# Moving modulation groups, squares and roots inside the loop over the recurrence's heads, in a two-block kernel on one core

## The reference, cut to what matters

```python
mod = (sc @ ada_w[l] + ada_b[l])[:, None, :]     # 9 rows of 1024: shift, scale, gate three times
...
hm = merge_heads(mlstm_chunkwise(q, k, v, log_i, log_f))                   # 4 heads of 128
out_m = head_rmsnorm(hm, mnorm_g, MLSTM_HEADS) * jax.nn.sigmoid(mo.astype(f32))
...
ho = merge_heads(hgrn2_chunkwise(hq_, hk_, hv_, hlf))                      # 4 heads of 128
out_h = head_rmsnorm(ho, hnorm_g, HGRN_HEADS) * jax.nn.silu(hg.astype(f32))
merged = jnp.concatenate([out_m, out_h], axis=-1).astype(y.dtype)
return merged @ w_out
```

## Time and profile before

| | |
|---|---|
| median of 3 runs | 1725.26 us (1725.07 to 1725.27) |
| profiled execution, its own time | 1724.61 us |
| span of the profiled execution | 1722.8 us |
| granted clock of PE over the span | 0.999 |
| loop (first `attend` to first transposition of the merged rows) | 346.55 to 386.04 us |
| busy over the span | PE 97%, DVE 66%, ACT 46%, POOL 21% |

### The profile page before, as it was taken

One profiled execution on the slowest core, in us unless ns is written; L12 is line 12 of the kernel. 1 busy time (PEld: TensorE's weight loads), 2 busy tenths in 40 slices (PEclk: granted clock), 3 DMA queues, 4 the chain that ended last, 5 costly groups with the idle time before them and its releaser, 6 DMA issues.

```text
span 1722.8 us, 32701 instructions
## 1 busy us (share of the span) xinstructions
PE 1678.9 (97%) x12702; PEld 1496.3 (87%) x12702; DVE 1142.6 (66%) x1883; ACT 789.4 (46%) x1239; POOL 354.7 (21%) x325
## 2 busy tenths in 40 slices
PE   6999999999999999999899999999999999999997
PEld 3999879977999889878779999999999988888886
DVE  4877867787555556874663899488899644444445
ACT  4433455655544454632243544555544433333334
POOL 2000100111000100000010767500000155555554
PEclk9999999999999999999999999999999999999999
DMA  9878855427565544430045455555555566666665
GB/s 361 291 268 306 303 226 180 147 103 277 172 216 173 195 137 145 155 131 11 27 171 173 125 175 179 164 159 159 159 161 158 177 191 193 193 195 192 189 193 169
DMA packets 64960, 314.40 MB, mean 182 GB/s; under 512 B 7216, under 2 KB 7632, under 8 KB 45776
## 3 DMA queue, kind: packets, MB, share of 16 engines
q1 hardware_dynamic: 63504, 305.94, 53.7%
q10 hardware_dynamic: 1280, 6.82, 1.1%
q0 software_dynamic: 64, 0.04, 0.0%
HBM read 311.72 MB, written 1.05 MB: 182 GB/s over the span
## 4 chain that ended last, share of the span: by engine, by line
PE 91%; DVE 3%; DMA 2%; ACT 1%; issue 1%; POOL 1%; SPq 0%; POOLq 0%; DVEq 0%; ACTq 0%
PE bank L421 26%; PE bank L423 25%; PE bank L422 25%; PE bank L2906 2%; DMA ring<-in_stream 2%; PE bank L2879 1%; DMA ring<-in_experts 1%; PE bank L2465 1%; PE bank L1447 1%; DVE ring_rounded L381 1%; PE bank L2478 1%; PE bank L857 1%; POOL ring_rounded L3212 1%; PE bank L2118 1%; PE bank L2132 0%
## 5 line engine op out<-in xcount | busy, mean ns | idle before, releaser
L423 PE MATMUL bank<-yb_rounded,ring_rounded 128*128 128x256 f32 x2032 | 574.8, 283 | 0.0
L2997 ACT CAST ring_rounded<-ring 128x1024 fp32r<-128x1024 f32 x248 | 260.5, 1051 | 287.1 <-DMA ring<-in_experts 287.1
L423 PEld LDWEIGHTS bank<-yb_rounded,ring_rounded 128*128 128x128 f32 x2032 | 389.5, 192 | 0.0
L381 DVE TENSOR_TENSOR ring_rounded<-ring,arena_rounded 128x1024 fp32r<-128x1024 f32 x230 | 272.8, 1229 | 105.2 <-ACT arena_rounded L367 104.5
L421 PE MATMUL bank<-yb_rounded,arena_rounded 128*128 128x256 f32 x1104 | 315.5, 286 | 2.2 <-issue 1.9
L422 PE MATMUL bank<-yT_rounded,arena_rounded 128*128 128x256 f32 x1104 | 312.6, 283 | 0.0
L3172 DVE TENSOR_TENSOR ring_rounded<-ring,ring_rounded 128x1024 fp32r<-128x1024 f32 x128 | 156.9, 1226 | 191.4 <-ACT ring_rounded L2997 191.4
L421 PE MATMUL bank<-yb_rounded,ring_rounded 128*128 128x256 f32 x960 | 278.2, 290 | 1.3 <-POOL ring_rounded L3212 0.5
L422 PE MATMUL bank<-yT_rounded,ring_rounded 128*128 128x256 f32 x960 | 271.3, 283 | 0.0
L367 ACT CAST arena_rounded<-ring 128x1024 fp32r<-128x1024 f32 x230 | 229.1, 1048 | 88.0 <-PE bank L421 77.5
L422 PE MATMUL bank<-ring_rounded,arena_rounded 128*128 128x512 f32 x688 | 268.0, 390 | 0.0
(11 more groups left out here) (447 smaller groups left out, 2608.3 us busy)
## 6 DMA issues: line engine op xcount, KB each, us to landing
ring<-in_stream SPq DMA_DIRECT2D x140, 1024.0 KB, 4.9
ring<-in_experts SPq DMA_DIRECT2D x256, 512.0 KB, 3.6
field<-in_stream SPq DMA_DIRECT2D x28, 512.0 KB, 7.1
field<-in_stream SPq DMA_DIRECT2D x4, 1024.0 KB, 8.4
yT<-in_stream SPq DMA_DIRECT2D x4, 512.0 KB, 5.5
field<-in_gains ACTq DMA_DIRECT2D x3, 512.0 KB, 7.9
field<-in_gains ACTq DMA_DIRECT2D x1, 1536.0 KB, 7.9
const<-in_const SPq DMA_DIRECT2D x1, 1473.0 KB, 11.8
```

Of the source, the lines that this page charges most:

```text
L381: ins = nc.vector.tensor_tensor(ring_r[:, g % SLOTS, half], ring[:, g % SLOTS, half], top.bitcast(F32), ALU.subtract)
L423: return first, pe.matmul(bank, s_rest, m_top, start=False, stop=stop)
L2997: nc.scalar.copy(expert_top[:, n % E_SLOTS, :], expert_w[:, n % E_SLOTS, :]).then_inc(expert_top_ready, 1)
```

## The change

It moves four things inside the loop; nothing is added or removed.

1. PE: in passes 2 and 4 the modulation groups stand ahead of `attend(i)` and `read_out(i - 1)`, not behind them. ACT's copy of their bank moves to match, to just behind `decay_exp(i + 1)`.
2. ACT: the eight squares of the mLSTM are taken four in pass 2 and four in pass 3, behind that pass's `head_square`, not all in pass 1 ahead of it.
3. ACT: the roots of the mLSTM are taken in pass 4, not pass 2.
4. DVE: their inverse is taken in pass 5, not pass 3.

```diff
@@ mix_pe
                 if i < HEADS * TT - 1:
                     decays(i + 1)
+                if i in LOOPED:
+                    ada_groups_pe(pe, LOOPED[i])
                 attend(i)
                 if i:
                     read_out(i - 1)
-                if i in LOOPED:
-                    ada_groups_pe(pe, LOOPED[i])
                 if i - 1 in LOOPED:
                     ada_sum_pe(pe, LOOPED[i - 1], but=3)
@@ mix_act
                 if i < last:
                     decay_exp(i + 1)
+                if i in LOOPED:
+                    ada_groups_act(act, LOOPED[i])
                 if i % TT:
                     bank = A.get(act)
                     nc.scalar.copy(cross[:, i // TT % 2, :], bank[:, 0:P]).then_inc(A.free, 1)
-                if i == 1:
-                    act.wait_ge(V.free, 4 + values_end["m"])
-                    for t in range(TT):
-                        for h in range(HEADS):
-                            ins = nc.scalar.activation(square_junk[:, t * HEADS + h, :], dm[:, h, t * P:(t + 1) * P], ACT.Square,
-                                                       accum_out=head_squares[:, t * HEADS + h:t * HEADS + h + 1])
-                    a(ins)
                 if 0 < i < last:
                     head_square(i - 1).then_inc(sem("h_squared"), 1)
                 if i == 2:
+                    act.wait_ge(V.free, 4 + values_end["m"])
+                if i in (2, 3):
+                    t = i - 2
+                    for h in range(HEADS):
+                        ins = nc.scalar.activation(square_junk[:, t * HEADS + h, :], dm[:, h, t * P:(t + 1) * P], ACT.Square,
+                                                   accum_out=head_squares[:, t * HEADS + h:t * HEADS + h + 1])
+                    a(ins)
+                if i == 4:
                     head_roots(0, 8).then_inc(sem("m_roots"), 1)
...
-                if i in LOOPED:
-                    ada_groups_act(act, LOOPED[i])
                 if i - 1 in LOOPED:
                     ada_sum_act(act, LOOPED[i - 1])
@@ mix_dve
-                if i == 3:
+                if i == 5:
                     dve.wait_ge(sem("m_roots"), 1)
                     vec.reciprocal(head_rstd[:, 0:8], head_root[:, 0:8]).then_inc(sem("m_rstd"), 1)
```

## The result

The changed kernel takes 1733.42 us (median of 6 runs, 1732.20 to 1733.59), the one before 1725.26 (6 runs, 1724.67 to 1725.42): 8.16 us more, ratio 1.0044 (95% interval 1.0033 to 1.0054; the two medians alone divide to 1.0047). The forecast was 1730.7 with a range up to 1732.0. The direction, and the place, were right; a third of the loss was not in the sum.

What follows compares the result with a forecast made beforehand. The prediction took PE as full in the loop, with DVE and ACT without slack ahead of attend(7). Roots 2.6 plus POOL's products 2.8 gave 5.4 us over 1725.26, forecast 1730.7 us, range 1727.6 to 1732.0.

Steps and rivals of the forecast that it cites:

- What bounds the kernel: In the loop: PE is full, DVE and ACT have no slack ahead of attend(7), so a late decay_exp(6) delays attend(7) equally.
- Groups on PE: PE, passes 2 and 4: groups cost 2.70 us in pass 4 before as after; PE stays full in either order, sum 0.
- term one: ACT, pass 4: table load, root and load back now stand between late head_square(3) and decay_exp(6), delaying attend(7) by 2.6 us.
- Squares: ACT, passes 2 and 3: moving the eight squares there from pass 1 has price 0 and gain 0.
- Term two: DVE, around decay(7): the later inverse makes POOL's products hold both L381 and L1767, 2.8 us in all.
- Behind the loop: After attend(7), merge, w_out and its chunk DMAs: nothing has slack to give back; put at 0, at most -0.3 us.
- Rival 4: ACT's table switches: a root starting well after its load costs another load's length each, 2.6 us more, 1733.3; chance 0.03.

Runs made afterwards that it cites:

- order_only: The kernel before with only the groups moved ahead of attend and read_out in passes 2 and 4, on PE and ACT; 1725.66 us, ratio 1.0005.
- order_undone: The changed kernel with the groups put back behind attend and read_out in passes 2 and 4, on PE and ACT; 1731.62 us, ratio 1.0035.
- nopool: The changed kernel without POOL's four products, a constant in their place (output not the reference's); 1729.59 us, ratio 1.0022.
- inverse_late: The kernel before with one edit: DVE takes the inverse of the roots in pass 5 instead of pass 3; 1729.45 us, ratio 1.0022.
- fill24: The changed kernel with 24 useless 128x128 products on PE ahead of attend(7), filling its wait; 1730.36 us, ratio 1.0025.
- nopool_fill: The changed kernel without POOL's four products and with 13 useless products on PE ahead of attend(7); 1727.79 us, ratio 1.0012.
- inverse_late_fill: The kernel before with the inverse in pass 5 and 17 useless products on PE ahead of attend(7); 1727.73 us, ratio 1.0011.
- squares_undone: The changed kernel with all eight squares of the mLSTM back in pass 1, ahead of head_square(0); 1732.26 us, ratio 1.0047.

## Why the prediction was wrong, step by step

- **What bounds the kernel**: right. PE full up to `attend(7)`, DVE and ACT without slack ahead of it; every experiment that made `decay_exp(6)` or DVE's pass 6 later moved `attend(7)`, and none that moved only earlier passes did so by more than about 0.5 us.
- **Groups on PE, "sum 0" by themselves**: measured +0.5 in the loop (order_only), in the noise. Their effect through `head_square(3)` was in term one, and order_undone shows it: 1.78 us.
- **Squares, 0**: measured 0.2.
- **Term one, roots, +2.6**: nopool gives 2.85 in the loop with the squares' 0.2 in it; the times of the loads, root and exponential came as worked out (374.82 less 0.3 of entry, for 374.14; the rest is that `read_out(3)` ended 0.4 us later than I had it, since `attend(4)` and the groups each carry a gap of 0.1 to 0.3 ahead of them).
- **Term two, POOL's products, +2.8**: changed less nopool 2.64; alone, in inverse_late, 2.47. The alternation of whole instructions, read from two waits of the trace before, was right, and so was the number of three waits; their place was off by one instruction. The working had POOL's first product start with the inverse (377.3), but it starts 0.34 us behind it (377.97, 378.31). So its second product came at 379.67, 0.08 us behind the first remainder (379.59), and waited for it, where the forecast had it 0.3 us ahead. The second remainder, L1768 and L1770 then paid, +0.85, +1.05 and +0.72, not the two remainders and L1768 with 0.7, 1.1 and 1.0. That the sums agree so well is in part luck.
- **Together**: 5.4 forecast, 40.24 - 34.75 = 5.49 measured; `attend(7)` was forecast "near 386.7", and came at 387.09 with 0.3 of that in the entry.
- **The step that failed** is "Behind the loop each step hangs on the one before ... I put it at 0". I had priced PE's idle time at its own length. PE idle for 5.82 us came back at half clock, and `attend(7)` and the read-outs took 2.75 us more. With this term the sum is 5.49 + 2.75 = 8.24, against 8.16 in the medians. fill24 takes it away alone, nopool_fill and inverse_late_fill take it away from each of the other terms.
- **Rival 4**, a table switch that costs more than its record, gave almost the measured time (1733.3) by a wrong reason: the root starts at 373.21 for a load that ends at 373.20, and the load back (1.28) at 373.53 with its exponential at 374.82. A number that fits is no evidence for its mechanism. So here, too, the drain of about 1380 ns of the Trainium skill ("ScalarE: Activation LUTs", "What ACT_TABLE_LOAD costs") is not seen.
- The profiled spans differ by 9.0 us, 0.8 more than the medians. 0.3 of it lies ahead of the loop and about 0.5 behind the start of the merge; what makes these was not followed up.

The Trainium skill has a rule that would have named the missing term: "TensorE: Matmul & The Clock Gate", section "Part 1: The HAM clock gate (the "warmup" mystery)", says that a gate halves the array's clock, from 2.4 to 1.2 GHz, when PE has been idle. This trace agrees, with 1.00 before the wait and 0.50 behind it.

## What to carry to other kernels

When a change adds idle time to a PE that was full, price two things: the wait, and the work behind it at the lower clock. Here waits of 3.15 us and more were each followed by 1.3 to 2.75 us of extra time, those of 1.75 and less by none; a single wait of 2.37 elsewhere was followed by a fall whose price was not taken apart. And before moving an instruction that releases POOL, look at which of DVE's instructions it will meet: the same four products cost nothing beside slack and 2.5 us on the path that PE waits for.

## What the runs showed that I had not expected

- The clock's fall is not strictly tied to the idle stretch. In nopool PE was idle 3.18 us, `attend(7)` began at 384.36, and the sixteen records took 3.17 us, between the 2.05 of the upper level and the 3.78 of the changed kernel: the fall came some 0.7 us later, while PE was working again (1.00 from 384 to 385, 0.53 from 385 to 386).
- Its price is no fixed number: 7.49, 6.37, 6.36, 6.28, 6.14 and 6.08 us for the stretch that takes 4.74 at full clock, and the longest idle time (5.82) and nearly the same one (5.81, squares_undone) gave 7.49 and 6.08. What sets it is how much of that work the low clock covers. The mean granted clock of these six stretches is 0.60, 0.73, 0.73, 0.74, 0.76 and 0.77, and length times clock is 4.5 to 4.7 us in each, beside 4.74 at 1.00. Why the clock came back later in the changed kernel's profiled execution than in the others no run shows; 2.75 us is the price in that one, and the fastest of the six (1732.20) may have paid less.
- Useless products made the changed kernel some 3 us faster (fill24), with the loop at the same length.
